# Half of the second layer's scale vector moved from TensorE matmuls into VectorE's chain of sums

## The reference

```python
mod = silu(cond) @ w_ada[l] + b_ada[l]          # 2048 -> 3 * 2048, for two conditions
shift, scale, gate = split(mod, 3)
h   = rmsnorm(x, norm_pre[l]) * (1 + scale) + shift
p   = h @ w_in[l]                               # 5120 columns
...                                             # attention and DFT mixing, or pooling and spatial gating
x   = x + gate * rmsnorm(concat @ w_out[l], norm_post[l])
```

## Time and profile before

| | |
|---|---|
| median of 3 runs | 1146.4 us (1146.11 to 1146.77) |
| profiled execution | 1148.2 us |
| its span, first to last instruction | 1146.4 us |
| TensorE busy | 1110.8 us, 97% |
| TensorE weight loads busy | 871.9 us, 76% |
| VectorE busy | 712.3 us, 62% |
| ScalarE busy | 414.1 us, 36% |
| mean DMA rate | 209 GB/s |

### The profile page before, as it was taken

How to read it: one execution, slowest core, us unless ns; L and a number is a source line. 1 busy time by engine, 2 the same in 40 slices (tenths; PEclk the granted TensorE clock), 3 DMA queues, 4 the chain that set the end, 5 groups by cost and what they waited for, 6 DMA issues and landing times.

```text
span 1146.4 us, 13756 instructions
## 1 busy us (share of the span) xinstructions
PE 1110.8 (97%) x5368; PEld 871.9 (76%) x5368; DVE 712.3 (62%) x978; ACT 414.1 (36%) x647; POOL 51.4 (4%) x100
## 2 busy tenths in 40 slices
PE   4999999999999999999999899999999999999997
PEld 2565677787787877788877688888878888788885
DVE  3545465778788785689974654566746765343335
ACT  4332333332455342233323872223333323233332
POOL 0000010000000001011110000000000000000000
PEclk8999999999999999999999899999999999999999
DMA  9988776465566577668758243455335556334323
GB/s 383 371 314 329 286 263 223 171 239 185 183 248 229 175 264 269 225 219 274 275 194 339 111 147 121 155 186 200 120 138 220 192 179 217 111 132 162 132 89 110
DMA packets 45359, 240.06 MB, mean 209 GB/s; under 512 B 5184, under 2 KB 5216, under 8 KB 25328
## 3 DMA queue, kind: packets, MB, share of 16 engines
q1 hardware_dynamic: 31024, 190.85, 44.7%
q0 software_dynamic: 11792, 44.09, 11.5%
q10 hardware_dynamic: 2480, 4.24, 1.2%
HBM read 235.47 MB, written 3.70 MB: 209 GB/s over the span
## 4 chain that ended last, share of the span: by engine, by line
PE 91%; DVE 3%; DMA 3%; ACT 2%; issue 1%; SPq 0%; DVEq 0%; ACTq 0%; POOLq 0%
PE bank L854 26%; PE bank L856 25%; PE bank L855 25%; PE bank L878 3%; PE bank L982 1%; DMA raw_first<-in_ada_first 1%; PE bank L786 1%; PE bank L941 1%; PE bank L965 1%; PE bank L1023 1%; PE bank L926 1%; DVE x L1352 1%; PE bank L993 1%; DMA third_raw<-in_w_ada 1%; PE bank L806 1%
## 5 line engine op out<-in xcount | busy, mean ns | idle before, releaser
L854 PE MATMUL bank<-w_hi,h_op 128*128 128x512 f32 x1116 | 457.3, 410 | 0.3
L856 PE MATMUL bank<-w_hi,h_op 128*128 128x512 f32 x1116 | 438.7, 393 | 0.0
L855 PE MATMUL bank<-w_lo,h_op 128*128 128x512 f32 x1116 | 437.1, 392 | 0.0
L1308 DVE TENSOR_TENSOR w_lo<-raw,w_hi 128x1024 fp32r<-128x1024 f32 x224 | 273.1, 1221 | 172.1 <-ACT w_hi L1060 171.9
L1060 ACT ACTIVATE w_hi<-raw 128x1024 fp32r<-128x1024 f32 x224 | 234.2, 1054 | 272.2 <-PE bank L856 253.8
L854 PEld LDWEIGHTS bank<-w_hi,h_op 128*128 128x128 f32 x1116 | 210.7, 189 | 72.6 <-issue 32.6
L856 PEld LDWEIGHTS bank<-w_hi,h_op 128*128 128x128 f32 x1116 | 210.3, 188 | 45.9
L855 PEld LDWEIGHTS bank<-w_lo,h_op 128*128 128x128 f32 x1116 | 211.0, 189 | 39.6 <-issue 0.7
L1477 DVE SCALAR_TENSOR_TENSOR wide<-wide_raw,cond,wide 128x1024 f32<-128x1024 f32 x80 | 101.7, 1276 | 0.8 <-DMA wide_raw<-in_w_ada 0.7
L854 PE MATMUL bank<-w_hi,o_low 128*128 128x512 f32 x192 | 75.9, 395 | 0.0
L856 PE MATMUL bank<-w_hi,o_low 128*128 128x512 f32 x192 | 74.9, 390 | 0.0
(11 more groups left out here) (194 smaller groups left out, 827.8 us busy)
## 6 DMA issues: line engine op xcount, KB each, us to landing
raw<-in_w_in SPq DMA_DIRECT2D x68, 1024.0 KB, 5.9
raw_first<-in_ada_first SPq DMA_DIRECT2D x32, 1024.0 KB, 7.2
raw<-in_w_ada SPq DMA_DIRECT2D x32, 1024.0 KB, 5.6
raw<-in_w_out SPq DMA_DIRECT2D x32, 1024.0 KB, 5.0
wide_raw<-in_w_ada POOLq DMA_DIRECT2D x44, 512.0 KB, 5.0
raw<-in_w_in SPq DMA_DIRECT2D x24, 512.0 KB, 6.5
third_raw<-in_w_ada POOLq DMA_DIRECT2D x20, 512.0 KB, 4.4
silu<-gate_rows ACTq DMA_DIRECT2D x16, 256.0 KB, 3.6
```

The source lines that it names most:

```text
L854: pe.matmul(out, operand(layer, kind, 0, k, t), hi, start=k == begin, stop=False)
L855: pe.matmul(out, operand(layer, kind, 0, k, t), lo, start=False, stop=False)
L856: last = pe.matmul(out, operand(layer, kind, 1, k, t), hi, start=False, stop=k == end)
L1308: dve.tensor_tensor(w_lo[:, half % WRING, :, :].rearrange("p k n -> p (k n)"), src, hi, ALU.subtract)\
```

## The change

The scale block of layer 1 is cut in two. Slices 0 to 7 stay with TensorE, 4 entries `ada`, now 18 steps apart from (3, 5). Slices 8 to 15 become 32 sums on VectorE and a fold, which is added to what `rows` holds. The three parts that are summed on VectorE (all of the gate, half of the scale, all of the shift) follow one another at a pace of 0.9 steps for each sum: the gate from (3, 9), folded at (7, 4); the scale's half from (7, 8), folded at (9, 6); the shift from (9, 6), folded at (13, 1). The three slots of the ring are taken in turn across the blocks, and `gate_store` of layer 0 goes from (8, 14) to (7, 6). 16 loads of 512 KB from GpSimd's queue take the place of 8 loads of 1 MB from SP's.

```diff
-WIDE = [(GATE_BLOCK[0], FIRST, 10, 12, 10), (SHIFT_BLOCK, FIRST + 5, 13, 10, 10)]
+SCALE_ADA = 8
+WIDE = [(GATE_BLOCK[0], 0, FIRST, 9, 9, 10), (SCALE_BLOCK, SCALE_ADA, FIRST + 4, 8, 9, 10),
+        (SHIFT_BLOCK, 0, FIRST + 6, 6, 9, 10)]
 WIDE_BLOCKS = [w[0] for w in WIDE]
+WIDE_FROM = {w[0]: w[1] for w in WIDE}
+SUMS = [(0, 0), (0, 1), (1, 0), (1, 1)]
...
+WIDE_LOADS = [(m, k, half) for m in WIDE_BLOCKS for k in range(WIDE_FROM[m], KT) for half in range(2)]
+THIRD_AGAIN = next(n for n, load in enumerate(WIDE_LOADS) if load[0] != GATE_BLOCK[0] and n % WIDE_RING == 1)
...
-    for n, (m, k) in enumerate(pairs):
-        put(FIRST, 5 + 14 * n, "ada", m, k, 2)
-    for m, c, s, step, per in WIDE:
-        for k in range(KT):
-            for j in range(4):
-                put(c, s + step * (4 * k + j) // per, "wide_sum", m, k, j // 2, j % 2)
-        put(c, s + step * 4 * KT // per + 2, "wide_fold", m)
+    for n, k in enumerate(range(0, SCALE_ADA, 2)):
+        put(FIRST, 5 + 18 * n, "ada", SCALE_BLOCK, k, 2)
+    for m, k0, c, s, step, per in WIDE:
+        for k in range(k0, KT):
+            for j, (half, n_cond) in enumerate(SUMS):
+                put(c, s + step * (4 * (k - k0) + j) // per, "wide_sum", m, k, half, n_cond)
+        put(c, s + step * 4 * (KT - k0) // per + 2, "wide_fold", m)
...
-    put(8, 14, "gate_store", 0)
+    put(7, 6, "gate_store", 0)
...
-        wide_slots = [wide_raw[:, 0, :], wide_raw[:, 1, :], third_raw[:, :]]
+        wide_slots = [wide_raw[:, 0, :], third_raw[:, :], wide_raw[:, 1, :]]
...
+            def load_wide(n):
+
+                m, k, half = WIDE_LOADS[n]
+                if n < WIDE_RING:
+                    wait_h(pool, 0, KT - 1)
+                else:
+                    m0, k0, half0 = WIDE_LOADS[n - WIDE_RING]
+                    pool.wait_ge(wide_summed[m0], 4 * (k0 - WIDE_FROM[m0]) + 2 * half0 + 2)
+                if n == THIRD_AGAIN:
+                    pool.wait_ge(gate_stored, 16 * N_OUT)
...
-            load_wide(GATE_BLOCK[0], 0, 2 * KT)
-            load_wide(SHIFT_BLOCK, 0, WIDE_RING - 1)
+            for n in range(2 * KT + 8):
+                load_wide(n)
 
             wait_full(pool, "pv", len(units) - 1)
             pool.dma_start(dft_sb[:, :], dft).then_inc(dft_in, 16)
             load_weight(1)
             load_bias(SHIFT_BLOCK)
-            load_wide(SHIFT_BLOCK, WIDE_RING - 1, 2 * KT)
+            for n in range(2 * KT + 8, len(WIDE_LOADS)):
+                load_wide(n)
...
                     wait_full(dve, *e)
-                    dve.wait_ge(bias_in, 16 * (BIAS_ORDER.index(m) + 1))
-
-                    wait_full(dve, *{0: ("first_cols", len(STAGES) - 1), 2: ("cols", SCALE_BLOCK)}[m])
-                    freed(dve.tensor_tensor(dst[:, :], side_bank(e)[:, :], bias_rows[:, :], ALU.add), e)
+                    if m == SCALE_BLOCK:
+
+                        wait_free(dve, *ada_entry[m, SCALE_ADA - 1])
+                        other = rows
+                    else:
+                        dve.wait_ge(bias_in, 16 * (BIAS_ORDER.index(m) + 1))
+
+                        wait_full(dve, *{0: ("first_cols", len(STAGES) - 1), 2: ("cols", SCALE_BLOCK)}[m])
+                        other = bias_rows
+                    freed(dve.tensor_tensor(dst[:, :], side_bank(e)[:, :], other[:, :], ALU.add), e)
```

More of the change, by code:

```diff
@@ L91 @@
 FIRST = 3
-WIDE = [(GATE_BLOCK[0], FIRST, 10, 12, 10), (SHIFT_BLOCK, FIRST + 5, 13, 10, 10)]
+SCALE_ADA = 8
+WIDE = [(GATE_BLOCK[0], 0, FIRST, 9, 9, 10), (SCALE_BLOCK, SCALE_ADA, FIRST + 4, 8, 9, 10),
+        (SHIFT_BLOCK, 0, FIRST + 6, 6, 9, 10)]
 WIDE_BLOCKS = [w[0] for w in WIDE]
+WIDE_FROM = {w[0]: w[1] for w in WIDE}
+SUMS = [(0, 0), (0, 1), (1, 0), (1, 1)]
 WIDE_RING = 3
-WIDE_LOADS = [(m, i) for m in WIDE_BLOCKS for i in range(2 * KT)]
-NTH_IN_SLOT = {(m, i): sum(j % WIDE_RING == i % WIDE_RING for _, j in WIDE_LOADS[:n])
-               for n, (m, i) in enumerate(WIDE_LOADS)}
+WIDE_LOADS = [(m, k, half) for m in WIDE_BLOCKS for k in range(WIDE_FROM[m], KT) for half in range(2)]
+THIRD_AGAIN = next(n for n, load in enumerate(WIDE_LOADS) if load[0] != GATE_BLOCK[0] and n % WIDE_RING == 1)
+NTH_WIDE = {load: n for n, load in enumerate(WIDE_LOADS)}
 BIAS_ORDER = [SCALE_BLOCK, GATE_BLOCK[0], SHIFT_BLOCK, GATE_BLOCK[1]]
@@ L286, in timetable @@
             put(c, s + 2 + j, "pool_mix", g, j)
-    pairs = [(m, k) for m in range(3) if m not in WIDE_BLOCKS for k in range(0, KT, 2)]
-    for n, (m, k) in enumerate(pairs):
-        put(FIRST, 5 + 14 * n, "ada", m, k, 2)
-    for m, c, s, step, per in WIDE:
-        for k in range(KT):
-            for j in range(4):
-                put(c, s + step * (4 * k + j) // per, "wide_sum", m, k, j // 2, j % 2)
-        put(c, s + step * 4 * KT // per + 2, "wide_fold", m)
+    for n, k in enumerate(range(0, SCALE_ADA, 2)):
[5 more added lines that the diff above has]
+        put(c, s + step * 4 * (KT - k0) // per + 2, "wide_fold", m)
     for half in range(2):
@@ L583, in first_drain @@
         def first_drain(m):
-            return ("wide_fold", m) if m in WIDE_BLOCKS else ada_entry[m, 0]
+            return ada_entry[m, 0] if (m, 0) in ada_entry else ("wide_fold", m)
         def half_ahead(p):
@@ L700, in load_bias @@
                 pool.dma_start(bias_rows[:, :], ada_rows[m]).then_inc(bias_in, 16)
-            def load_wide(m, first, last):
-                layer, third = BLOCKS[m]
[L705 to L717, removed]
+            def load_wide(n):
[7 more added lines that the diff above has]
+                    pool.wait_ge(gate_stored, 16 * N_OUT)
+                layer, third = BLOCKS[m]
+                col = third * D + LANES * half
+                pool.dma_start(wide_slots[n % WIDE_RING], w_ada[layer, k * P:(k + 1) * P, col:col + LANES])\
+                    .then_inc(wide_in[n % WIDE_RING], 16)
             def load_weight(n):
@@ L894, in side_product @@
                     pe.wait_ge(fold_in, 16)
-                    pe.wait_ge(wide_summed[e[1]], 4 * KT)
+                    pe.wait_ge(wide_summed[e[1]], 4 * (KT - WIDE_FROM[e[1]]))
                     for c_ in range(2):
@@ L912, in side_product @@
                     else:
-                        wait_free(pe, *(("wide_fold", e[1]) if e[1] in WIDE_BLOCKS else ada_entry[e[1], KT - 1]))
+                        wait_free(pe, "wide_fold", e[1])
                     for i in range(4):
@@ L1459, in part @@
                     m, k, half, c_ = e[1:]
-                    n = 4 * k + 2 * half + c_
+                    n = 4 * (k - WIDE_FROM[m]) + SUMS.index((half, c_))
                     cols = slice(LANES * half, LANES * (half + 1))
-                    slot = (2 * k + half) % WIDE_RING
-                    src = wide_slots[slot]
-                    dve.wait_ge(wide_in[slot], 16 * (NTH_IN_SLOT[m, 2 * k + half] + 1))
+                    load = NTH_WIDE[m, k, half]
+                    src = wide_slots[load % WIDE_RING]
+                    dve.wait_ge(wide_in[load % WIDE_RING], 16 * (load // WIDE_RING + 1))
                     if n == 0:
@@ L1471, in part @@
                             wait_full(dve, "wide_fold", WIDE_BLOCKS[WIDE_BLOCKS.index(m) - 1])
-                    if k == 0:
+                    if k == WIDE_FROM[m]:
                         dve.tensor_scalar(wide[:, c_, cols], src, cond[:, k, c_:c_ + 1], None, ALU.mult)\
```

## The result

The changed kernel takes 1148.72 us in the median of 15 runs (1146.81 to 1150.22), beside 1146.77 us for the kernel before (15 runs, 1145.89 to 1147.65). The ratio is 1.0017 with a 95% interval of 1.0010 to 1.0024, so it is slower by 1.1 to 2.8 us.

A forecast was written before the change was run, and what follows sets the result against it. TensorE was taken to set the time, with VectorE keeping up by a narrow margin. Terms -7.8 + 1.95 + 1.9 + 0.7 + 0.7 = -2.55 us took the 1146.4 us median to 1143.9, range 1140.8 to 1147.4 for 8 in 10.

The forecast's parts named there:

- TensorE's gain: On TensorE, eight pairs become four (-7.8 us) and one fold is added (+1.95 us): 5.85 us less work.
- The price of 1.95: On TensorE, a pair costs 1.95 us: 2.18 us between main matmuls where one alone takes 0.23; a fold the same.
- rival 3: TensorE not the bound, removed pairs hidden under weight loads: 1146.4 plus the stalls, up to 1149.7; chance 0.05.
- Chunk 8: Sums ahead of two splits make TensorE late by 1.2 and 0.7 us: 1.9 us, bounds nothing and 3.9.
- Chunks 10 to 12: Four more sums by (12, 3), less VectorE's waits and the split's slack: 0.7 us lost, ends 0 and 1.5.
- `gate_store` and the added loads: Store moved to (7, 6) and 16 added loads: 0 each, though slow landings may cost a few tenths.
- Attention: Chunks 3 to 7: 0.7 us lost, at the copy of pv in chunk 6 with 1.25 us of slack.
- Elsewhere in the stretch I take nothing: Rest of chunks 3 to 7: 0, since chunk 6's 6.7 us of VectorE waits fit five sums, chunks 4 and 5 more.
- Rival 2: VectorE becomes the bound in attention, chunks 4 to 6 losing 6 us beyond the 0.7: 1149.9; chance 0.12.
- the forecast's own case: Whole kernel: stalls of 1 to 6 us in all, time from 1141.5 to 1146.5; chance 0.63.

The follow-up runs named there:

- experiment 2: Kernel before with the last four pairs of the scale (slices 8 to 15) left out and nothing in their place: ratio 0.9923, 8.8 us faster than before.
- experiment 3: Changed kernel with every sum but the first of each block's four run on 512 of its 1024 columns: ratio 0.9940, 6.9 us faster than before.
- experiment 5: Changed kernel with the gate's last three sums one step later each: ratio 1.0007 to the kernel before, about 1 us faster than the changed kernel.
- experiment 4: Changed kernel with its four pairs 14 steps apart instead of 18: ratio 0.9998 to the kernel before, about 2 us faster than the changed kernel.
- experiment 7: Changed kernel with sums placed by hand, doubled only in chunk 9, and pairs at (3, 5), (4, 3), (5, 15), (6, 15): 1142.49 us, ratio 0.9956 to before.

## Why the prediction was wrong

The forecast was 1143.9 us and a small gain; it became a small loss, and the range ended at 1147.4, below the median of 1148.7.

**TensorE's gain: right.** 5.85 us were forecast, and the chunks without losses show it: chunk 5 is 2.1 us shorter, and experiment 2 gives 2.04 us for a pair in chunk 6 and 2.15 in the mean of four. The price of 1.95 was a little low: at 2.04 us, and about as much for a fold, the work is 6.1 us less and 7.4 us are lost. TensorE was the bound. The weight loads are busy 76% as before, and each removed pair still gave its full price. The Trainium skill (Perfetto Trace Analysis, Identifying the Most-Contended Engine) says to judge TensorE's headroom by the arithmetic done against the peak and by the busy share of the weight loads, as measures of how close a kernel is to the chip's peak. Taken as the time that removed matmuls would not give back, which is how I used it for rival 3, experiment 2 does not bear it out.

**Chunk 8: right.** 1.9 us forecast, 1.8 found, at steps 4 and 6 as named (1.3 and 0.6 where 1.2 and 0.7 were reckoned), with the split as the thing waited for.

**Chunks 10 to 12: the number right, the place not.** 0.7 us were forecast, at (12, 3), and 0.9 found, but chunk 12 lost nothing. 0.65 went in chunk 10 (steps 5, 11 and 12) and 0.2 in chunk 11, in pieces under 0.3 us. They are gone with shorter sums (experiment 3), so VectorE's time is the cause, but that 0.7 and 0.9 agree is luck.

**`gate_store` and the added loads.** 0 was forecast and 0 found in the changed kernel's profile, and experiment 3 bears it out. The profiles of experiments 4 and 5 have 2.2 and 1.8 us lost in chunks 11 and 12 beside waits for such loads, so the term is not safely 0 in every run.

**Attention: the step that failed.** The prediction took 0.7 us for chunk 6, and then "Elsewhere in the stretch I take nothing." The 0.7 us came as reckoned: step (6, 8) is 0.65 us longer. What failed is the nothing elsewhere, 2.8 us in chunk 4 and 1.7 in chunk 7; the whole stretch lost 4.9 us. Three parts of the reasoning were wrong.

- I counted VectorE's idle time in the stretch as room ("In chunk 6 as a whole VectorE waits 6.7 us, and five more sums need 6.0"). A wait for something that hangs on VectorE's own earlier result moves with it. At (7, 1) VectorE's 1.45 us of waiting came through ScalarE from its own `neg_max`; experiment 5 took one sum away ahead of it, and TensorE's wait fell by just that sum. Rival 2 came nearest to this, with 6.7 us in attention where 4.9 came, and got 0.12.
- I took the copy of pv in chunk 6, with 1.25 us of slack, for the tightest place that gets sums ahead of it. The one at (7, 1) had 0.06 us before the change, and gets two sums ahead of it. I looked in one chunk only; the earlier trace rows even had a wait of 0.8 us for such a copy, at (6, 2), so places without slack were on the page. In chunk 4 two sums, a rotation and the copy of pv follow one another, and my rows had no line of that place.
- I treated the pairs only as work to be saved. The one at (4, 3) covered VectorE's rotation, and moving it four steps cost 2.4 us in chunk 4, 0.9 of them its own wait at the new place (experiment 4). I had the new table before me and priced nothing for this move.

The range was too narrow at the top for the same reason: its upper end had chunk 8 and chunks 10 to 12 at their limits, but only "some loss" in attention. Rival 2, VectorE as the bound in attention, should have been priced in part within the forecast's own case.

## What to carry to other kernels

When work moves to an engine that is 85% to 97% busy in a stretch, price it place by place: what stands ahead of each result that the bound engine waits for, with no credit for waits that hang on the late engine itself. Two pieces in one short step cost more than the same work spread, and a table that gives out work at 0.9 steps has such doubles at places nobody chose; here the same instructions placed by hand turned 2 us lost into 3 to 5 us gained. A piece of work on the bound engine can also be the cover for its neighbour, so where it is moved, ask who was catching up behind it. Not every place gains by such cover: of three pairs placed for it in experiment 7, one helped.

## What was not expected

A move of pairs alone, with no instruction more or less, was worth 2.4 us in one chunk (52.34 to 49.97 us). Four pairs less took 8.6 us and not 7.8 from the stretch: a pair costs 2.0 to 2.1 us and not 1.95, and 0.3 us came at one place, the steps (9, 3) and (9, 4). With shorter sums the stretch from chunk 3 to chunk 13 became 6.9 us shorter, where TensorE's work explains 6.1: the kernel before was not free of VectorE's lateness either. Step (6, 2), where the one wait of 0.8 us stood, went from 4.14 to 3.39 us.
